# Memory keys projected feature-major: weights stationary, 256 memory tokens moving

## The reference, cut to what matters

```
for i in range(DEPTH):                                        # DEPTH = 2
    kv = rmsnorm(mem_prompt, mem_norm[i]) @ w_mem_kv[i]       # 256 x 1024 @ 1024 x 2048
    mk.append(kv[..., :1024].reshape(B, 256, 4, 256))         # keys
    mv.append(kv[..., 1024:].reshape(B, 256, 4, 256))         # values

def cross_attn(q, mem_k, mem_v):
    s = einsum('bthd,bmhd->bhtm', q, mem_k) * 256 ** -0.5
    return einsum('bhtm,bmhd->bthd', softmax(s), mem_v)
```

## Time and profile before

| | us |
|---|---|
| median of 3 runs | 1373.97 |
| lowest, highest | 1372.78, 1380.74 |
| the profiled execution, device time | 1380.12 |
| its span, first to last instruction | 1378.3 |
| PE busy in the span | 1247.1 |
| mean granted TensorE clock | 0.954 of full speed |

### The profile page before, as it was taken

The page is one execution under the profiler, slowest core; times in us unless marked ns, Lnnn a source line. Parts: engine busy times, 40 slices in busy tenths (PEclk is TensorE's granted clock), DMA queues, the critical chain, the costliest instruction groups (busy, mean ns, idle before and its releaser), DMA issues.

```text
span 1378.3 us, 13810 instructions
## 1 busy us (share of the span) xinstructions
PE 1247.1 (90%) x5950; PEld 742.4 (54%) x5950; DVE 363.7 (26%) x877; ACT 152.8 (11%) x344; POOL 42.5 (3%) x58
## 2 busy tenths in 40 slices
PE   6999998989989998869999998999899989888776
PEld 3477776766334343347676675553677753333223
DVE  3221113022122222331223122336400041223224
ACT  2000002012111100011110201000200021001001
POOL 0000000000000000000000001223000000000000
PEclk9999999998999999979999999999999959989998
DMA  9743348631799999973232323579984417999993
GB/s 398 280 153 122 129 163 340 264 148 61 284 429 424 428 429 427 427 322 122 88 136 112 122 77 137 209 296 355 374 338 163 179 45 325 427 427 428 427 427 135
DMA packets 27265, 364.54 MB, mean 264 GB/s; under 512 B 3152, under 2 KB 3168, under 8 KB 5056
## 3 DMA queue, kind: packets, MB, share of 16 engines
q1 hardware_dynamic: 23904, 338.92, 60.9%
q10 hardware_dynamic: 1696, 18.88, 3.3%
q0 software_dynamic: 1600, 5.81, 1.0%
HBM read 339.27 MB, written 24.32 MB: 264 GB/s over the span
## 4 chain that ended last, share of the span: by engine, by line
PE 71%; DMA 22%; DVE 3%; issue 1%; ACT 1%; POOL 0%; DVEq 0%; SPq 0%; POOLq 0%; ACTq 0%
PE bank L623 25%; DMA ring<-in_gu 22%; PE bank L429 11%; PE bank L330 8%; PE bank L486 4%; PE bank L760 4%; PE bank L476 2%; PE bank L517 2%; PE bank L316 1%; PE bank L442 1%; PE bank L747 1%; PE bank L352 1%; PE bank L385 1%; PE bank L495 1%; PE bank L408 1%
## 5 line engine op out<-in xcount | busy, mean ns | idle before, releaser
L623 PE MATMUL bank<-hT,ring 128*128 128x288 f32 x1408 | 346.6, 409 | 8.9 <-DVE hT L1012 3.3
L623 PEld LDWEIGHTS bank<-hT,ring 128*128 128x128 f32 x1408 | 268.8, 191 | 87.2 <-issue 8.5
L486 PE MATMUL bank<-ring,arena 128*32 128x512 f32 x1024 | 135.5, 668 | 51.5 <-DMA ring<-in_gu 49.7
L429 PE MATMUL bank<-arena,ring 128*128 128x288 f32 x640 | 155.7, 406 | 1.8 <-DVEq L1076 1.8
L429 PEld LDWEIGHTS bank<-arena,ring 128*128 128x128 f32 x640 | 121.4, 190 | 35.6 <-issue 2.2
L330 PE MATMUL bank<-ring,arena 128*128 128x512 f32 x256 | 111.2, 594 | 3.1 <-DVE arena L1012 3.1
L486 PEld LDWEIGHTS bank<-ring,arena 128*32 128x32 f32 x1024 | 33.1, 117 | 146.5 <-DMA ring<-in_gu 78.4
L476 PE MATMUL bank<-arena 128*128 128x512 f32 (+1 forms) x192 | 102.9, 664 | 1.8 <-DVE arena L1142 1.1
L330 PEld LDWEIGHTS bank<-ring,arena 128*128 128x128 f32 x256 | 48.2, 190 | 63.4 <-issue 61.9
L476 PEld LDWEIGHTS bank<-arena 128*128 128x128 f32 (+1 forms) x192 | 33.1, 199 | 72.6 <-issue 71.1
L517 PE MATMUL bank<-arena 128*128 128x288 f32 x256 | 70.1, 420 | 2.1 <-issue 1.7
(11 more groups left out here) (201 smaller groups left out, 816.5 us busy)
## 6 DMA issues: line engine op xcount, KB each, us to landing
ring<-in_gu SPq DMA_DIRECT2D x64, 2048.0 KB, 24.6
ring<-in_dn SPq DMA_DIRECT2D x32, 2048.0 KB, 17.7
ring<-in_rin SPq DMA_DIRECT2D x14, 2048.0 KB, 8.6
ring<-in_wkv SPq DMA_DIRECT2D x8, 2048.0 KB, 17.7
ring<-in_cin SPq DMA_DIRECT2D x8, 2048.0 KB, 9.3
ring<-in_kc SPq DMA_DIRECT2D x8, 2048.0 KB, 8.6
ring<-in_vc SPq DMA_DIRECT2D x8, 2048.0 KB, 11.5
ring<-in_st SPq DMA_DIRECT2D x8, 2048.0 KB, 8.2
```

Of the source, the lines that this page charges most:

```text
L429: mm = pe.matmul(bank[1 + o % 4][:, 0:T], w[:, k, :], cat[:, k, :], start=(k == 0), stop=(k == kt - 1))
L486: mm = pe.matmul(bank[2][32 * e:32 * e + 32, :], xt[:, k, 32 * e:32 * e + 32], wv[:, e, kk, :], start=(k == 0), stop=(k == KD - 1), skip_g ...
L623: mm = pe.matmul(outs[o], w[:, o, k, :], src[:, k, :], start=(k == 0), stop=(k == KD - 1))
```

## The change

Keys and values part ways in `memory_kv`. For the keys (slots 0 and 1) a 128x128 piece of the weights is now stationary and the 256 memory tokens of `hm` move. A block is two feature blocks (o = 0, 1) of 256 tokens, each with eight matmuls of 256 columns into its half of one bank: the result is a quarter of `KT` as it stands. ACT copies each bank into `KT`. `Ktok`, `keys1`, `turn_keys`, `keys_turned`, the transposes and the second set of copies are gone, and so are the waits on them, among them PE's in packs 1 and 3. The stores of the keys go out from `KT` in its own layout (8 KB for a partition), and the host turns that output. The wait for layer 0's key store moves from ACT's first copy of `qx` (which shared its place with `Ktok`) to `keys_ahead`, where `KT` is overwritten. The values are done as before.

```diff
@@
-            KT_BANKS = ((0, 1, 2, 3), (4, 7, 4, 7))
@@ def memory_kv(i, j):  (PE)
+                if c < 2:
+                    for o in range(2):
+                        f = (2 * mb + o) * P
+                        for k in range(KD):
+                            if i == 0 and j == 0 and o == 0:
+                                pe.wait_ge(S("normed"), k + 1)
+                            mm = pe.matmul(bank[KV_BANKS[i][j]][:, o * NM:(o + 1) * NM], w[:, k, f:f + P],
+                                           src[:, k, :], start=(k == 0), stop=(k == KD - 1), skip_group_check=True)
+                    mm.then_inc(S("kv_sum"), 1)
+                    return
                 for k in range(KD):
-                    if i == 0 and j == 0:
-                        pe.wait_ge(S("normed"), k + 1)
                     mm = pe.matmul(bank[KV_BANKS[i][j]][:, :], src[:, k, mb * P:(mb + 1) * P], w[:, k, :],
                                    start=(k == 0), stop=(k == KD - 1))
                 mm.then_inc(S("kv_sum"), 1)
-
-            def turn_keys(i, groups):
-                src = (Ktok, keys1)[i]
-                for g in groups:
-                    for hd in range(2):
-                        for mb in range(2):
-                            mm = pe.transpose(bank[KT_BANKS[i][g]][:, hd * 256 + mb * P:hd * 256 + (mb + 1) * P],
-                                              src[:, mb, (2 * g + hd) * P:(2 * g + hd + 1) * P], C("ident"))
-                    mm.then_inc(S("kt_turned"), 1)
@@ def experts(L):  (PE)
-                    if L == 0 and i in KEYS_IN:
-                        pe.wait_ge(S("gt_out"), i)
-                        turn_keys(1, KEYS_IN[i])
-                        pe.wait_ge(S("kt_out_a"), 2 + KEYS_IN[i][1] + 1)
@@ (PE, ahead of the convolution's projection)
-            pe.wait_ge(S("ktok_out"), 4)
-            turn_keys(0, range(4))
-
-            pe.wait_ge(S("kt_out_a"), 2)
-            pe.wait_ge(S("kt_out_d"), 2)
+            pe.wait_ge(S("kt_out"), 4)
             pe.wait_ge(S("v_out"), 4)
             pe.wait_ge(S("normed"), NORM_DONE["mix0"])
@@ def memory_kv():  (ACT)
                 for j in range(4):
                     act.wait_ge(S("kv_sum"), j + 1)
-                    act.activation(Ktok[:, j % 2, (j // 2) * 512:(j // 2 + 1) * 512], bank[j][:, :], ACT.Copy) \
-                       .then_inc(S("ktok_out"), 1)
-                for g in (1, 3):
-                    act.wait_ge(S("kt_turned"), g + 1)
-                    act.activation(KT[:, 2 * g:2 * g + 2, :], v3(bank[g][:, :], 2), ACT.Copy) \
-                       .then_inc(S("kt_out_a"), 1)
+                    act.activation(KT[:, 2 * j:2 * j + 2, :], v3(bank[j][:, :], 2), ACT.Copy).then_inc(S("kt_out"), 1)
@@ def keys_ahead():  (ACT)
+                act.wait_ge(S("keys_stored0"), 16)
                 for j in range(4):
                     act.wait_ge(S("kv_sum"), 8 + j + 1)
-                    act.activation(keys1[:, j % 2, (j // 2) * 512:(j // 2 + 1) * 512],
-                                   bank[(4, 7, 0, 1)[j]][:, :], ACT.Copy).then_inc(S("kv1_out"), 1)
+                    act.activation(KT[:, 2 * j:2 * j + 2, :], v3(bank[(4, 7, 0, 1)[j]][:, :], 2), ACT.Copy) \
+                       .then_inc(S("kv1_out"), 1)
                 act.wait_ge(S("kv1_out"), 4)
-                act.dma_start(a["out_mk"][1].rearrange("(m p) n -> p m n", p=P), keys1) \
+                act.dma_start(a["out_mk"][1], KT) \
                     .then_inc(S("keys_stored1"), 16)
@@ def memory_kv():  (DVE)
-                for g in (0, 2):
-                    dve.wait_ge(S("kt_turned"), g + 1)
-                    dve.tensor_copy(KT[:, 2 * g:2 * g + 2, :], v3(bank[g][:, :], 2)).then_inc(S("kt_out_d"), 1)
@@ def store_memory():  (POOL)
-                pool.wait_ge(S("ktok_out"), 4)
-                pool.dma_start(a["out_mk"][0].rearrange("(m p) n -> p m n", p=P), Ktok).then_inc(S("keys_stored0"), 16)
+                pool.wait_ge(S("kt_out"), 4)
+                pool.dma_start(a["out_mk"][0], KT).then_inc(S("keys_stored0"), 16)
```

More of the change, by code:

```diff
@@ L56 @@
 VALUES_IN = {2: 2, 4: 3}
-KEYS_IN = {1: (0, 1), 3: (2, 3)}
 def pack_sequence(l):
@@ L150, in build @@
         hm0 = v3(ar(CATO + 2048, KD * NM), KD)
-        Ktok = v3(ar(PHO, 2048), 2)
-        keys1 = v3(hT_[:, 0:2048], 2)
         qx = v3(ar(PHO, 8 * T), 8)
@@ L833, in store_state @@
                     .then_inc(S(f"state_stored{b % 2}"), 16)
[L835 to L839, removed]
             def attention(i):
@@ L899, in experts @@
                         values_ahead(VALUES_IN[i])
-                    if L == 0 and i in KEYS_IN:
-                        keys_turned(KEYS_IN[i])
                     act.wait_ge(S("gt_turned"), PACKS * L + i + 1)
@@ L931, in _ @@
                 act.wait_ge(S("cin_sum"), 4 * c + 4)
-                if c == 0:
-                    act.wait_ge(S("keys_stored0"), 16)
                 act.activation(qx[:, c, :], bank[4 * (c % 2) + 3][:, 0:T], ACT.Copy).then_inc(S("qx_out0"), 1)
@@ L1304, in _ @@
             experts(0)
-            dve.wait_ge(S("keys_stored1"), 16)
             norm("mix1", xT, ((hT, "mix1"),), T)
@@ L1466 @@
 OUTS = {"out_y": (P, KD, T), "out_cvp": (P, 8, 2), "out_cvs": (P, 8, 16), "out_rp": (H, P, 2, DV),
-        "out_rs": (NB, P, 8, DV), "out_mk": (2, NM, D), "out_mv": (2, NM, D)}
+        "out_rs": (NB, P, 8, DV), "out_mk": (2, P, KD, NM), "out_mv": (2, NM, D)}
 def feature_major(v, k):
@@ L1569, in unpack @@
     rs = r["out_rs"].reshape(NB, P, H, 2, DV).transpose(0, 2, 3, 1, 4).reshape(1, NB, H, 256, DV)
-    mk = r["out_mk"].reshape(2, 1, NM, H, 256)
+    mk = r["out_mk"].transpose(0, 3, 2, 1).reshape(2, 1, NM, H, 256)
     mv = r["out_mv"].reshape(2, 1, NM, H, 256)
```

## The result

| | before | after |
|---|---|---|
| median of 22 runs, in us | 1376.13 | 1365.36 |
| lowest, highest | 1368.65, 1383.55 | 1355.53, 1372.47 |
| ratio to before, 95% interval | | 0.9919, 0.9900 to 0.9938 |
| the profiled execution, device time | 1380.12 | 1359.51 |
| its span | 1378.3 | 1357.3 |

The change makes the kernel faster by 10.8 us, 0.8% (the interval is 8.5 to 13.8 us). The forecast was 1.2 us.

A forecast was written before the change was run, and what follows sets the result against it. PE's own work bounds the front and route, DMA bytes the stretches around packs 1 and 3. Terms -1.66 + 0.44 = -1.22 us took a median of 1373.97 to 1372.7; forecast 1371.5 to 1374, range 1368 to 1380.

The forecast's parts named there:

- The last of the prediction's own signs of being wrong: Behind layer 0's last pack: forecast wrong if the unexplained 5.50 us before L316 changed by more than the -1.22 us sum.
- The front, -1.66 us: Program start, layer 0: without key transposes and copies, the projection begins at 75.20 in place of 76.86, gaining 1.66 us.
- 256 columns, +0.44 us: Key matmuls of both layers: 128 records of 256 columns replace 64 of 512, costing +0.22 us a layer, loads hidden.
- The first of the two statements that were weighed: Key matmuls: loads hide only for other row groups; its rival of exposed loads: +24.3 us, 1397, chance 0.03.
- The packs, 0: Layer 0's expert packs 1 and 3: 1.83 us of PE work removed from each, hidden by saturated DMA; gain taken as 0.
- The route, the stores, the waits at nothing: Layer 0's route keeps its order, +0.22 us for widths only; key stores and moved or already met waits cost 0.
- A shift elsewhere: Rival: unexplained pieces, such as 5.50 us before L316, outweigh the change; median near 1380 or 1368; chance 0.13.

## Why the prediction was wrong

The direction was right, the size was not, and the time fell below the range (1368). The last of the prediction's own signs of being wrong came true: the 5.50 us before L316 changed by more than the sum.

*The front, -1.66 us.* Right: -1.60. By the times DVE's copy of the values is what PE waits for, though the profile names no releaser there.

*256 columns, +0.44 us.* Right: +0.32. The weight loads stay hidden; the nearest row (L385, 0.2163) was a good price, 0.2169 measured in the route. The first of the two statements that were weighed, of the Trainium skill, "TensorE: Matmul & The Clock Gate", Part 3, What overlaps and what doesn't, no overlap within the same row groups, does not hold for this stream.

*The packs, 0.* Right, by the traces with and without the transposes. (The waits of 2.46 and 1.31 us in the earlier trace rows are those of pack 2's gate-up, behind pack 1, not of pack 1 itself; the argument stands.) *The route, the stores, the waits at nothing.* Nothing in the traces speaks against them. So the direct effect, of the steps that were priced, is 1.3 us. No comparison of runs resolves it (the kernels with the stall stand at 1.0008 with an interval of 0.9984 to 1.0031, those without at 0.9919 and 0.9937); it is read from the traces alone.

*"A shift elsewhere"*, the 5.50 us ahead of L316. This is the step that failed. I had them in front of me, called them something that nothing in the profile explains, left them in the sum unchanged without a reason, and let them stand only in a rival at 0.13, with a median near 1368 as its far end. That rival names no cause and leaves out the tail, so that one such piece did shrink is luck and no credit to it. They were 9.6 us with their tail: a fixed wait of this program, for a page of instructions, whose cause the change does touch. The change alters the number of PE's instructions, and so where the branch behind the packs and its target lie in pages.

How much of this was to be had before the run? The packets of q8 and the stall itself, behind a branch, were there to be seen. The count alone doesn't show it: it puts the target in the next page, and only the stall says that the kernel before sits in the unlucky band, where with 299 instructions from branch to target 43 of the 256 offsets of the branch put the target two pages on. But given that, moved by 192 from any offset in that band, the target is in the next page. So a rival "the change removes the 5.50 us" with a price and a high chance could have been worked out; that it was more than a theory took the runs. The rule behind it is a page of the Trainium skill ("Runtime: NRT & Kernel Launch", Instruction fetch mechanics) that I did not weigh.

The second part of the failure is the tail. Even with the stall put at 5.50, the 4.1 us behind it (norm sum and projection at the lower clock) belong to it.

## What to carry to other kernels

An "issue" gap in the chain behind a branch need not be noise: look for a packet of the instruction queue that lands just before PE goes on, and count where branch and target lie. An edit that changes the number of instructions ahead of a branch can switch such a stall on or off, so compare two versions with the branch at the same offset, or move its target by code that never runs, before you credit the edit. Here the stall with its tail makes up 9.6 us in the traces, of a gain of 10.8, and the kernel before reaches the changed one's time with 64 instructions fewer in a pass that is skipped.

## What was not expected of the hardware

- A page of instructions that PE waits for took 5.3 to 5.6 us on the chain while weights moved at some 425 GB/s, and 2.12 us with the DMA engines idle. What the load adds is the time before the packet begins (3.6 to 3.9 us against 0.67). PE goes on 1.5 to 1.7 us after the packet has landed, either way.
- 6.48 and 6.58 us of an idle PE cost it 4.1 and 4.3 us more at the lower clock afterwards, but 6.29 us in another run only 1.6. With 1.95 and 2.73 us of idle time (stalls of 0.97 and 1.76) the norm sum took 1.7 us more and the projection behind it 1.7 less. What sets this stays open.
- Empty instructions with a semaphore increment took PE 0.15 us each: 16 more of them moved its first matmul from 10.72 to 13.16 us.
